# Stick-breaking attention on one core: the values products of both heads issued as a pair, in every second step

## The reference

```python
def block(args):                       # one block of queries, all heads
    z = jnp.einsum('bhqd,bshd->bhqs', qblk, kf)
    mask = kpos[None, :] < tq[:, None]
    log_keep = jnp.where(mask, jax.nn.log_sigmoid(-z), 0.0)
    after = lax.cumsum(log_keep, axis=3, reverse=True) - log_keep
    a = jnp.where(mask, jnp.exp(jax.nn.log_sigmoid(z) + after), 0.0)
    return jnp.einsum('bhqs,bshd->bhqd', a, vf)
```

## Time and profile before

| | |
|---|---|
| median of 3 runs | 3112.95 us (3112.75 to 3118.0) |
| the profiled execution | 3124.41 us, its span 3121.2 us |
| TensorE busy | 2987.4 us, 96% |
| VectorE / ScalarE / GpSimd busy | 1492.0 / 948.7 / 769.8 us |
| mean granted TensorE clock | 0.972 |
| one sweep | 62.5 to 62.7 us, four of them |

### The profile page before, as it was taken

One profiled execution on the slowest core, in us unless ns is written; L12 is line 12 of the kernel. 1 busy time (PEld: TensorE's weight loads), 2 busy tenths in 40 slices (PEclk: granted clock), 3 DMA queues, 4 the chain that ended last, 5 costly groups with the idle time before them and its releaser, 6 DMA issues.

```text
span 3121.2 us, 37530 instructions
## 1 busy us (share of the span) xinstructions
PE 2987.4 (96%) x13944; PEld 2315.2 (74%) x13944; DVE 1492.0 (48%) x1743; ACT 948.7 (30%) x1524; POOL 769.8 (25%) x502
## 2 busy tenths in 40 slices
PE   6999999999999999999999999999999999899998
PEld 5887875556677777778888888877777777677766
DVE  6454564554433435364343444333264454466654
ACT  4323235665300012331122211122134234244441
POOL 4302112222233321123333333322201101300025
PEclk9999999999999999999999999999999999798999
DMA  6101000000211110011111111112100001000023
GB/s 224 53 15 34 28 21 14 9 20 19 81 49 44 47 38 26 29 34 47 47 47 47 47 47 47 47 41 81 36 15 14 22 1 36 6 6 6 1 103 120
DMA packets 166350, 128.72 MB, mean 41 GB/s; under 512 B 19264, under 2 KB 150048, under 8 KB 165968
## 3 DMA queue, kind: packets, MB, share of 16 engines
q1 hardware_dynamic: 164816, 118.55, 12.5%
q10 hardware_dynamic: 1408, 8.50, 0.7%
HBM read 114.20 MB, written 12.65 MB: 41 GB/s over the span
## 4 chain that ended last, share of the span: by engine, by line
PE 65%; DVE 5%; issue 2%; ACT 2%; DMA 1%; SPq 0%; POOL 0%; DVEq 0%; ACTq 0%; POOLq 0%
PE ps L705 17%; PE ps L707 16%; PE ps L706 16%; PE ps L2745 4%; PE ps L2584 3%; PE ps L618 2%; PE ps L2835 1%; PE ps L2837 1%; PE ps L2836 1%; PE ps L2643 1%; PE ps L2644 1%; PE ps L2645 1%; PE ps L644 0%; DVE probs_low L2185 0%; PE ps L701 0%
## 5 line engine op out<-in xcount | busy, mean ns | idle before, releaser
L705 PE MATMUL ps<-NH,w_high 128*128 128x512 f32 (+1 forms) x1992 | 779.9, 392 | 21.1 <-POOL w_low L1016 6.7
L706 PE MATMUL ps<-NL,w_high 128*128 128x512 f32 (+1 forms) x1992 | 781.2, 392 | 0.0
L707 PE MATMUL ps<-NH,w_low 128*128 128x512 f32 (+1 forms) x1992 | 778.5, 391 | 0.0
L1014 POOL CAST w_high<-w_raw 128x1024 fp32r<-128x1024 f32 x193 | 208.4, 1080 | 2169.7 <-PE ps L707 1191.0
L1016 POOL TENSOR_TENSOR w_low<-w_raw,w_high 128x1024 fp32r<-128x1024 f32 x193 | 480.9, 2492 | 15.4
L705 PEld LDWEIGHTS ps<-NH,w_high 128*128 128x128 f32 x1992 | 379.4, 190 | 115.3 <-issue 19.9
L706 PEld LDWEIGHTS ps<-NL,w_high 128*128 128x128 f32 x1992 | 378.9, 190 | 83.5
L707 PEld LDWEIGHTS ps<-NH,w_low 128*128 128x128 f32 x1992 | 379.3, 190 | 82.7
L769 DVE TENSOR_TENSOR hT<-hT,ps 128x1024 f32<-128x1024 f32 x168 | 205.1, 1221 | 250.2 <-PE ps L707 250.2
L705 PE MATMUL ps<-act_high,w_high 128*128 128x512 f32 x352 | 141.4, 402 | 2.9 <-DVE act_low L1886 2.9
L707 PE MATMUL ps<-act_high,w_low 128*128 128x512 f32 x352 | 139.4, 396 | 0.0
(11 more groups left out here) (400 smaller groups left out, 5335.9 us busy)
## 6 DMA issues: line engine op xcount, KB each, us to landing
w_raw<-in_w_in SPq DMA_DIRECT2D x69, 512.0 KB, 3.8
w_raw<-in_w_up SPq DMA_DIRECT2D x44, 512.0 KB, 3.8
w_raw<-in_w_out SPq DMA_DIRECT2D x24, 512.0 KB, 3.3
w_raw<-in_w_down SPq DMA_DIRECT2D x22, 512.0 KB, 3.8
w_raw<-in_w_xkv SPq DMA_DIRECT2D x8, 512.0 KB, 5.9
x_in<-in_x SPq DMA_DIRECT2D x8, 512.0 KB, 9.2
residual_spill<-hT SPq DMA_DIRECT2D x1, 4096.0 KB, 13.5
hT<-residual_spill ACTq DMA_DIRECT2D x1, 4096.0 KB, 13.0
```

Source lines behind the costliest of these rows:

```text
L705: nc.tensor.matmul(o, wh, xh, start=start, stop=False)
L706: nc.tensor.matmul(o, wh, xl, start=False, stop=False)
L707: return nc.tensor.matmul(o, wl, xh, start=False, stop=stop)
L1014: nc.gpsimd.tensor_copy(WH[slot][:, :], w_raw[slot][:, :]).then_inc(w_high, 1)
```

## The change

TensorE issues no product in even steps. In an odd step n, from 3 on, it issues product(n - 3) and product(n - 2) directly behind each other: the same key block for head 0 and head 1, whose results go to rows 0 to 63 and 64 to 127 of the same bank. Nothing else is moved on any engine, and no buffer is added.

```diff
@@ -2480,7 +2480,8 @@
                             scores(n + 2)
                         if n == 2:
                             wait_freed(pe, SB, i, J + 3)
-                        if n >= 2:
+                        if n >= 3 and n % 2:
+                            products(n - 3)
                             products(n - 2)
                         if n == 0:
                             wait_bank(pe, SB, i, U + 3)
```

## The result

The changed kernel takes 3129.01 us (median of 6 runs, 3125.75 to 3135.53), before 3117.69 us in the same comparison (3112.75 to 3123.82). The ratio is 1.0035, 95% interval 1.0018 to 1.0051: slower by 0.35%, 11 us (6 to 16). Forecast were 3117 us, +4 us, and a range of 3108 to 3124; the time lies above it. Of the 12 us between 3117 and 3129, 4.7 are before's own: the forecast stood on its median of 3 runs, 3112.95, and with the other three it is 3117.69.

A forecast was written before the change was run, and what follows sets the result against it. Sweeps were taken as bound by whichever arrives last at the sums, TensorE or DVE's soft_low. Terms 0.29 + 0.51 + 0.40 - 0.6 + 0.43 gave +1.0 us per sweep, 4 over four: 3112.95 + 4 = 3117 us, range 3108 to 3124.

The forecast's parts named there:

- The bound of a sweep: In the four sweeps, neither TensorE alone nor the chain over ACT and DVE; whichever reaches the sums last decides each step.
- What the pairing saves: On TensorE, a pair of 512 columns takes 1.51 us where two products take 2.00; per pair 0.7 saved in all.
- What it costs by its place: Two products ahead of the sums in odd steps, none in even ones: odd steps lengthen by 0.51 us at 512 columns.
- the walk: Step-by-step count through one sweep of who reaches the sums last: +1.0 us per sweep, 4 us over four; chance 0.55.
- steps 7, 13, 17 and 23: Odd steps of a sweep where the second product delays the sums: +0.29, +0.51, +0.40 and +0.43 us.
- the win in steps 17 to 21: Steps held by TensorE before; 0.4 to 0.79 us per sweep can be won back, taken as -0.6.
- rival 4: Uneven load in the sweeps lets TensorE's clock fall; called small, no size given; chance 0.25 shared with the no-overlap case.
- Rival 1: A pair's products don't overlap: 1.91 us a pair, 2.5 to 3.1 per sweep, +11, 3124; chance 0.25 including a clock fall.
- Rival 2: TensorE's work decides and the chain has slack: 6 us saved per sweep, 24 in all, 3089; chance 0.12.

The follow-up runs named there:

- even_left_out: The kernel before with the products of even units 0 to 20 left out and nothing in their place; ratio to before 1.0028.
- wide_pairs: The changed kernel with pairs from unit 12 on only, single products in each step before that, as in before; ratio to before 1.0010.
- pair_apart: The changed kernel with one full-width bf16 matmul of 128 columns between the two products of a pair, so they can't overlap; ratio to before 1.0065.
- pair_fill: The changed kernel plus filler matmuls on an unused bank in even steps 2 to 22, where products were taken away; ratio to before 1.0006.
- the filled kernels: Kernels with pairs, all or only the wide ones, plus filler matmuls in TensorE's idle steps, against before; ratios 0.9990 to 1.0023.

## Why the prediction was wrong

**The bound of a sweep** was read rightly: neither TensorE alone nor the chain. TensorE's wait before the sums grew from the 79.7 us of the earlier trace rows as forecast, in sum over engine and weight loads and over the narrow steps at half clock too:

```profile
  DVE sb_soft_low L1707: 115.6, 130
```

**What the pairing saves** was mis-sized. From the earlier trace rows I took the second product to start beside the second matmul of the first, 1.51 us for a pair of 512; it is 1.00. Those rows showed a product that was late for its `aS`, and so a bound from above, not the cost.

**What it costs by its place**: with the pair at 1.51 the walk gave +0.29, +0.51, +0.40 and +0.43 in steps 7, 13, 17 and 23. With a pair no longer than a product these terms are nothing, and what is left is the win in steps 17 to 21, put at 0.6. Measured at full clock: -0.85 a sweep (61.35 against 62.2). The changed kernel itself has full clock from step 13 on. Its sums(13), (17), (21) and (23):

```profile
485.68 0.50 PE L2443 MATMUL ps<-sb_soft_high,neg_tri_r 128*128 128x512 f32 x1
...
496.12 0.50 PE L2443 MATMUL ps<-sb_soft_high,neg_tri_r 128*128 128x512 f32 x1
...
507.63 0.49 PE L2443 MATMUL ps<-sb_soft_high,neg_tri_r 128*128 128x512 f32 x1 [0.43 <-DVE sb_soft_low L1707]
...
512.52 0.50 PE L2443 MATMUL ps<-sb_soft_high,neg_tri_r 128*128 128x512 f32 x1
```

Against 480.70, 491.40, 503.25 and 508.34 in the earlier trace rows, steps 17 to 21 win 0.34 us, about half of what the walk gave; 0.26 come from steps 13 to 17 and 0.20 from 21 to 23, where it had losses. The sum from sums(13) to (23) is 26.84 us, just what even_left_out has without these products: here the chain over ACT and DVE sets the time, as the walk said. The walk had its mechanism right and its terms too large. That the total came out slower, as it said, is luck: the place that it gave as the reason costs nothing here.

**The step that failed is rival 4**: "The idle stretches of the even steps are around 1 us, and the clock stayed at 1.00 through a loop with stretches like it; small." That before kept its clock was taken to mean that it had room to spare. It had little: TensorE had been busy for 7.65 us of the first 9.6 in before, where the clock held, and for 7.17 in the changed kernel, where it fell to 1.2 GHz right behind; and with before's own steps it fell in one sweep of wide_pairs. The price was never worked out. It is 65.45 - 61.35 = 4.1 us a sweep, 16.4 in all, and 3.4 of it is covered by the pairs' gain: 13.0.

**The rivals.** Rival 1, no overlap, gave 3124 and 65.5 us for a sweep, near to what was measured, and would have been believed on the sweep's length alone. The row of step 19 refutes it for this kernel, and pair_apart, with a matmul put in between, has 4.0 where the rival had 2.5 to 3.1. Rival 2, TensorE's work decides, is out: of the 6 us per sweep of work (5.8 with the columns of the eleven pairs that change, where the sum took those of twelve), 0.85 came through at full clock, so DVE and ACT hold the even steps, as the walk had it. In steps 16 to 22 the even step starts its sums 2.3 to 2.7 us after the odd one's; in all four it waited for soft_low, 0.43 to 0.93 us. Only step 14 follows without a wait, after 1.9 us, and step 15 then waits for 0.93.

**The range** ended at 3124 because the clock's fall was put together with rival 1 at one price.

What stays open: why the clock held in some sweeps and fell in others behind the same work (wide_pairs, pair_fill, pair_apart), and where the 3.6 us go that the filled kernels win in their sweeps. Their totals scatter by 10 us or more from run to run, as before's do. Before's go with the mean clock, 3122.9 to 3128.9 us in the runs at 0.969 and 3110.4 to 3115.5 in those at 0.975, while its sweeps repeat, so this lies outside the sweeps. An interval of 0.13% to either side doesn't resolve 0.12%.

## What to carry to other kernels

Where an engine is idle for part of a stretch and its clock is still up, ask whether it can spare the busy time before making its work cheaper or moving it into fewer steps: here the clock took 4.1 us of a sweep where the overlap won 0.85. That the clock held in one trace doesn't say that there was room, as the third sweep of wide_pairs shows. Look at the granted clock of the stretch itself, per stage and in every repetition, not at the kernel's mean. And a row in which an instruction was late for its data gives a bound on what it costs when it isn't, never the cost.

## What the runs showed of the hardware that was not expected

- Two float32 products of 64 columns of weights each, into rows 0 to 63 and 64 to 127 of one bank, take 1.00 us together, as one does, although each is two matmuls and both of the first product's stand ahead of the second's in the code. With a full-width matmul of 128 columns between the two it is 2.17 us.
- Leaving out 44 matmul calls made the kernel 0.28% slower: at full clock its steps were shorter (26.84 against 27.64 us from sums(13) to (23)), and the clock in its sweeps was 0.90 to 0.95.
- The kernel before is near that edge too: with its own steps 0 to 13, one sweep in four of wide_pairs fell to half clock 7.5 us in, for 6.8 us, behind the same 5.81 us of work as the one that held.
- A loop body made longer by fillers once came with a stop of 4.35 us at the loop's end; that the one caused the other isn't shown.
